# Half of a triangular inverse moved from GpSimd to VectorE, its stores and loads re-ordered, and one wait of the final loads changed

## The reference

```python
m = jnp.where(strict, jnp.einsum('nbhik,nbhjk->nbhij', kb, kc) * decay, 0.0)
rhs = jnp.concatenate([vc * bc[..., None], kb * jnp.exp(G)[..., None]], axis=-1)
sol = lax.linalg.triangular_solve(m + jnp.eye(C, dtype=m.dtype), rhs,
                                  left_side=True, lower=True, unit_diagonal=True)
...
y = y + jnp.einsum('tef,efd->td', act, p['w_exp_down'][gi])
...
x = x + hier_moe(rmsnorm(x, p['norm_ffn']), p)
return (rmsnorm(y_p, norm_final), ...)
```

## Time and profile before

| | us |
|---|---|
| runs: median (lowest to highest) | 1358.15 (1356.75 to 1359.48) |
| profiled execution: its time | 1358.79 |
| its span, first to last instruction | 1357.0 |
| busy: PE, PEld, DVE, ACT, POOL | 1266.0, 986.7, 480.5, 424.2, 217.6 |
| mean granted TensorE clock | 0.978 |

### The profile page before, as it was taken

How to read it: one execution, slowest core, us unless ns; L and a number is a source line. 1 busy time by engine, 2 the same in 40 slices (tenths; PEclk the granted TensorE clock), 3 DMA queues, 4 the chain that set the end, 5 groups by cost and what they waited for, 6 DMA issues and landing times.

```text
span 1357.0 us, 23622 instructions
## 1 busy us (share of the span) xinstructions
PE 1266.0 (93%) x10186; PEld 986.7 (73%) x10186; DVE 480.5 (35%) x798; ACT 424.2 (31%) x730; POOL 217.6 (16%) x295
## 2 busy tenths in 40 slices
PE   5999999999999999959999897999999999999996
PEld 4999997888999998859999796544445444444543
DVE  5441353433346656423344776211111111111113
ACT  5532225433243567513456552001001010110004
POOL 0450000000122212830111054010000001000003
PEclk9999999999999999979999997999999999999997
DMA  5234339441262134332113249799999999999987
GB/s 225 94 109 151 117 130 367 157 181 68 89 220 74 63 102 123 114 101 86 55 40 111 105 165 376 315 398 424 430 430 432 431 431 430 430 430 430 431 333 173
DMA packets 68521, 317.91 MB, mean 234 GB/s; under 512 B 30143, under 2 KB 38719, under 8 KB 45521
## 3 DMA queue, kind: packets, MB, share of 16 engines
q1 hardware_dynamic: 66137, 312.80, 59.1%
q0 software_dynamic: 2304, 3.94, 0.8%
HBM read 296.07 MB, written 25.10 MB: 237 GB/s over the span
## 4 chain that ended last, share of the span: by engine, by line
PE 64%; DMA 20%; DVE 5%; ACT 5%; POOL 2%; issue 2%; SPq 1%; POOLq 0%; ACTq 0%; DVEq 0%
PE pp L957 31%; DMA e_up<-in_w_up 17%; PE pp L1134 14%; PE pp L1123 3%; PE pp L1007 2%; DMA yt<-y_rows 1%; PE pp L1333 1%; DVE w_l L2108 1%; PE pp L1353 1%; PE pp L927 1%; POOL inv_s L1968 1%; POOL inv L1973 1%; PE pp L1361 1%; ACT w_h L1537 1%; DMA raw<-in_w_blk 1%
## 5 line engine op out<-in xcount | busy, mean ns | idle before, releaser
L957 PE MATMUL pp<-ht_h,w_h 128*128 128x260 f32 x1248 | 262.1, 291 | 0.6 <-DVE w_l L2108 0.6
L957 PE MATMUL pp<-ht_h,w_l 128*128 128x260 f32 x1248 | 252.3, 284 | 0.0
L957 PE MATMUL pp<-ht_l,w_h 128*128 128x260 f32 x1248 | 252.1, 284 | 0.0
L957 PEld LDWEIGHTS pp<-ht_h,w_h 128*128 128x128 f32 x1248 | 193.4, 190 | 5.0 <-issue 3.6
L957 PEld LDWEIGHTS pp<-ht_l,w_h 128*128 128x128 f32 x1248 | 193.4, 190 | 0.0
L957 PEld LDWEIGHTS pp<-ht_h,w_l 128*128 128x128 f32 x1248 | 193.4, 190 | 0.0
L2108 DVE TENSOR_TENSOR w_l<-raw,w_h 128x2048 fp32r<-128x2048 f32 x52 | 122.3, 2351 | 100.9 <-ACT w_h L1537 100.9
L1134 PE MATMUL pp<-e_up,xt 128*64 128x512 f32 x512 | 114.9, 602 | 16.7 <-DMA e_up<-in_w_up 16.7
L1123 PE MATMUL pp<-sel,h2p 104*128 104x128 bf16 x1920 | 114.7, 222 | 2.6 <-DVE sel L2560 2.6
L1537 ACT ACTIVATE w_h<-raw 128x2048 fp32r<-128x2048 f32 x52 | 99.6, 1916 | 47.4 <-PE pp L957 43.4
L1134 PE MATMUL pp<-e_gate,xt 128*64 128x512 f32 x512 | 112.6, 592 | 1.4 <-DVE xt L2607 1.4
(11 more groups left out here) (443 smaller groups left out, 1699.3 us busy)
## 6 DMA issues: line engine op xcount, KB each, us to landing
e_gate<-in_w_gate SPq DMA_DIRECT2D x15, 4096.0 KB, 20.8
e_down<-in_w_down SPq DMA_DIRECT2D x28, 2048.0 KB, 14.3
e_up<-in_w_up SPq DMA_DIRECT2D x14, 4096.0 KB, 22.6
raw<-in_w_blk SPq DMA_DIRECT2D x52, 1024.0 KB, 5.2
kv_ring<-in_cache_k SPq DMA_DIRECT2D x8, 1024.0 KB, 6.6
kv_ring<-in_cache_v SPq DMA_DIRECT2D x8, 1024.0 KB, 4.8
s_ring<-in_state_gdn SPq DMA_DIRECT2D x16, 512.0 KB, 5.0
e_up<-in_w_up SPq DMA_DIRECT2D x3, 2048.0 KB, 17.8
```

Source lines behind the costliest of these rows:

```text
L957: last = mm(dst, w_[:, k, cs], x_[:, k, ts], start=(k == 0 and q == 0), stop=(k == KD - 1 and q == 2))
```

## The change

- The column steps become two helpers, `column_product` and `column_out`, that either engine can issue. GpSimd keeps steps 0 to 14 (`SOLVE_SPLIT` is 15), VectorE does 15 to 30, three to five steps a gap, and turns the inverse right after the last one; `inv_turn` is no event any more.
- In `gap(0)` and `gap(1)` the solve now stands ahead of `conv_s` and `sd_u`; `zero` moves from `gap(2)` to `gap(1)`.
- SyncE asks for the first chunk's `m_t` rows between the two stores, waits for the first store alone before it loads blocks, loads the four of `t_lo` first, and those of `t_up` after the second store. `mt4` waits for `t_lo` alone, `tx4` for `t_up`, each by a count of its own (two old semaphores are used again, from 16 and from 32 on).
- The final row loads wait for `oh_mm` in place of `quarter_mm`.

```diff
-    gap(0, ("conv_s", 1), ("solve", 15, 18))
-    gap(1, ("sd_u",), ("solve", 18, 22))
-    gap(2, ("zero",), ("solve", 22, 26), ("turn_v", 0))
-    gap(3, ("solve", 26, 31), ("inv_turn",))
+    gap(0, ("solve", 15, 18), ("conv_s", 1))
+    gap(1, ("zero",), ("solve", 18, 22), ("sd_u",))
+    gap(2, ("solve", 22, 26), ("turn_v", 0))
+    gap(3, ("solve", 26, 31))
...
+        def column_product(tt, j):
+            n, m = 31 - j, j + 1
+            return tt(inv_s[:, 0:n * m].rearrange("p (n m) -> p n m", n=n),
+                      a32[:, j, j + 1:32].rearrange("p (n o) -> p n o", o=1).to_broadcast([128, n, m]),
+                      inv[:, j, 0:m].rearrange("p (o m) -> p o m", o=1).to_broadcast([128, n, m]), ALU.mult)
+
+        def column_out(tt, j):
+            n, m = 31 - j, j + 1
+            below = inv[:, j + 1:32, 0:m]
+            return tt(below, below, inv_s[:, 0:n * m].rearrange("p (n m) -> p n m", n=n), ALU.subtract)
...
-                sp.wait_ge(t_zero, 2 * c + 1)
-                for i, dst in ((1, t_up[c % 2]), (0, t_lo)):
-                    if i == 0:
+                sp.wait_ge(t_zero, 2 * c + (1 if c else 2))
+                for i, dst in ((1, t_up[c % 2]), (0, t_lo)) if c else ((0, t_lo), (1, t_up[0])):
+                    if c and i == 0:
                         sp.wait_ge(t_zero, 2 * c + 2)
+                    if not c and i == 1:
+                        sp.wait_ge(turn_stored, turn_from + 16)
...
                     sp.dma_start(inv_rows[0], inv[:]).then_inc(inv_stored, 16)
+                    load_chunk_rows(0)
                     sp.wait_ge(inv_done, SOLVED + 1)
-                    sp.dma_start(inv_rows[1], inv_t[:]).then_inc(inv_stored, 16)
+                    sp.dma_start(inv_rows[1], inv_t[:]).then_inc(turn_stored, 16)
...
-                        sp.wait_ge(inv_stored, 32)
+                        sp.wait_ge(inv_stored, 16)
...
             sp.wait_ge(y_free, rounds * NPAIR + 1)
-            sp.wait_ge(quarter_mm, rounds)
+            sp.wait_ge(oh_mm, rounds)
...
-                pe.wait_ge(t_loaded, 128 * (n + 1))
+                pe.wait_ge(t_loaded, 64 * (n + 1))
...
+                pe.wait_ge(up_loaded, up_from + 64 * (n + 1))
                 each(("tx4", n), fn)
...
-                elif e == "inv_turn":
-                    dve.wait_ge(inv_done, SOLVED)
-                    copy(inv_t[:], inv[:].rearrange("p i k -> p k i")).then_inc(inv_done, 1)
+                elif e == "solve" and ev[1] >= SOLVE_SPLIT:
+                    for j in range(ev[1], ev[2]):
+                        dve.wait_ge(inv_done, 2 * j)
+                        column_product(tt, j).then_inc(inv_done, 1)
+                        dve.wait_ge(inv_done, 2 * j + 1)
+                        column_out(tt, j).then_inc(inv_done, 1)
+                    if ev[2] == 31:
+                        dve.wait_ge(inv_done, SOLVED)
+                        copy(inv_t[:], inv[:].rearrange("p i k -> p k i")).then_inc(inv_done, 1)
```

More of the change, by code:

```diff
@@ L281 @@
 EU_EXTRA = 32
-SOLVED = 62
+SOLVED, SOLVE_SPLIT = 62, 15
 TOK_UNIT = (0, 1, 3, 0, 1)
@@ L545, in build_step @@
         t_zero, t_loaded = sem("t_zero"), sem("t_loaded")
+        up_loaded, up_from = mem_loaded, 16
+        turn_stored, turn_from = ws_loaded, 32
         m_loaded = [sem(f"m_loaded{i}") for i in range(2)]
@@ L711, in load_inverse, with load_chunk_rows @@
                         own = slice(32 * b + NH * c, 32 * b + NH * c + NH)
-                        sp.dma_start(dst[blk, :, blk], inv_rows[i, own].rearrange("h i k -> i h k")).then_inc(t_loaded, 16)
+                        sp.dma_start(dst[blk, :, blk], inv_rows[i, own].rearrange("h i k -> i h k"))\
+                            .then_inc(up_loaded if i else t_loaded, 16)
+            def load_chunk_rows(c):
+                sp.dma_start(m_t[c % 2][:], m_rows[NH * c:NH * c + NH].rearrange("h j i -> j h i"))\
+                    .then_inc(m_loaded[c % 2], 16)
             xk = a["x_t"].rearrange("p (k n) -> p k n", k=KD)
@@ L794, in _ @@
                     sp.dma_start(inv_rows[0], inv[:]).then_inc(inv_stored, 16)
+                    load_chunk_rows(0)
                     sp.wait_ge(inv_done, SOLVED + 1)
-                    sp.dma_start(inv_rows[1], inv_t[:]).then_inc(inv_stored, 16)
+                    sp.dma_start(inv_rows[1], inv_t[:]).then_inc(turn_stored, 16)
                 elif e == "t_load":
                     if ev[1] == 0:
-                        sp.wait_ge(inv_stored, 32)
+                        sp.wait_ge(inv_stored, 16)
                     load_inverse(ev[1])
-                elif e == "m_load":
+                elif e == "m_load" and ev[1]:
                     c = ev[1]
@@ L804, in _ @@
                         mmed(sp, ("ss", c - 2))
[L805 to L808, removed]
+                    load_chunk_rows(c)
                 elif e == "late_loads":
@@ L1202, in experts @@
                                 last.then_inc(y_mm, 1)
-                        if f == 0:
-                            last.then_inc(quarter_mm, 1)
                         if f == nf - 1:
@@ L1576, in tile @@
                     if t >= 5:
-                        act.wait_ge(inv_stored, 32)
+                        act.wait_ge(inv_stored, 16)
+                        act.wait_ge(turn_stored, turn_from + 16)
                     fn(whole(zg[:, t, :]), ps, ACT.Sigmoid, bias=param("b_gate", t + 8)).then_inc(free, 1)
@@ L1958, in _ @@
                     nc.gpsimd.memset(inv[:].rearrange("p i k -> p (i k)")[:, 0:1024:33], 1.0).then_inc(zeroed, 1)
-                elif e == "solve":
+                elif e == "solve" and ev[1] < SOLVE_SPLIT:
                     if ev[1] == 0:
```

10 lines of the change are left out of this document (2 added, 8 removed).

## The result

| | before | after |
|---|---|---|
| median of 4 runs beside each other, us | 1358.49 | 1342.26 (1340.09 to 1344.16) |
| ratio, 95% interval | | 0.9881 (0.986 to 0.9903) |
| profiled execution: time, span, us | 1358.79, 1357.0 | 1343.78, 1341.5 |
| mean granted TensorE clock | 0.978 | 0.987 |

The changed kernel is 16.2 us faster; 19.7 was forecast.

What follows compares the result with a forecast made beforehand. The chain was taken as 64% TensorE and 20% DMA, with re-ordering winning only at the wait for the inverse and the tail. Middle 14.4 plus tail 5.3 made 19.7 us: 1358.15 to 1338.5, range 1333 to 1347.

Steps and rivals of the forecast that it cites:

- The solve: Columns 15 to 30 on VectorE take 12.3 us; the inverse is finished at 581.3, 6.05 us before 587.35.
- the memsets wouldn't block the columns: GpSimd's three memsets beside VectorE's columns were taken at nothing; if they held VectorE up, 2.88 us.
- ScalarE's cover: ScalarE's exponentials, delayed 5.3 us, end at 584.95, just ahead of VectorE's a_t product at 585.05: covered by 0.1 us.
- The store and t_lo: Inverse's store lands 2.56 us after 581.3; the last lower block load, issued at 585.25, lands at 587.0, perhaps 588.
- The merge: First merge product on TensorE starts at 588.0 instead of 599.44, 11.4 us sooner.
- The clock: From the merge's start to 605.4 TensorE ran 6 us at half clock; 3.0 us more gained if the clock holds.
- The prediction's worry: TensorE's two new waits for ScalarE, 3 to 3.5 us each, may lower the clock; the second could cost about 2 us.
- Middle: From the solve through the merge, sooner merge start and held clock together give 14.4 us.
- The tail: Stored rows asked for sooner at the end move as a block from about 1315: 5.3 us, between 1.2 and 9.4.
- The named sign: If the last down product stretches beyond 7.1 us, stored rows and expert weights take turns on the queue.
- The slower rival: VectorE's column steps cost 2.4 times, as beside a GpSimd column; merge 8.4 us late, 1361.3 us; chance 0.04.

Runs made afterwards that it cites:

- e1: Changed kernel with the final row loads again waiting for the first quarter of the last down product (quarter_mm); 1346.03 us, 0.9894 of the kernel before.
- e6: Changed kernel with the store of the turned inverse moved behind the four t_lo loads; 1340.93 us, 0.9847 of the kernel before.
- e7: Changed kernel with each share of the stored rows loaded as 96 and 8 partitions instead of one load of 104; 1340.51 us, 0.9847 of the kernel before.
- e10: Changed kernel timed again, unchanged, in a later group of runs; 1340.86 us, 0.9862 of the kernel before.
- e2: Kernel before with the division of the columns alone, stores, loads and row request in the old order; 1350.0 us, 0.9931 of the kernel before.
- e9: Kernel before with unused products in TensorE's two waits, 90 before the sample norm's matmul and 28 before the merge; 1361.46 us, 1.0007 of the kernel before.
- e4: Changed kernel with the sample convolution ahead of columns 15 to 17 in VectorE's order; 1343.59 us, 0.9877 of the kernel before.
- e5: Changed kernel with the sample convolution ahead of the columns and 24 unused products in TensorE's wait before the sample norm; 1337.67 us, 0.9833 of the kernel before.
- e11: Changed kernel with convolution first, 24 unused products before the sample norm, and the turned inverse stored behind the t_lo loads; 1339.52 us, 0.9845 of the kernel before.
- e12: Kernel before with unused products in TensorE's two waits, 90 before the sample norm's matmul and 52 before the merge; 1357.04 us, 0.9973 of the kernel before.
- e8: Changed kernel with four 128x1024 products of x_mid by itself on GpSimd behind the three memsets; 1345.0 us, 0.99 of the kernel before.

## Why the prediction was right, point by point

- **The solve**: 15.6 us from column 14 to the finished inverse were forecast; it took 14.6. The seven small steps of the sample state took 1.7 us instead of 2.2, the columns and the convolution the rest less. (Rows 11 give 1.02 ns an element, not the 1.03 that I used; that is 0.1 us of it.) That the memsets wouldn't block the columns was right; that the turning's 1.63 held the price of a memset beside it I did not see.
- **ScalarE's cover** failed. It was to hold by 0.1 us; `a_t` waited 1.28, and 1.24 to 1.28 in e1, e6, e7 and e10. ScalarE was as late as forecast; VectorE, 1 us sooner with the inverse and 0.6 with the turning, came to it earlier. So this ate what VectorE won beyond the forecast: `a_t` is 6.4 us sooner relative to column 14, 6.1 were forecast.
- **The store and t_lo** were mis-sized: 3.21 and 3.47 us in the first trace instead of 2.56 and 1.75, the second with perhaps 1 us more for `inv_t`'s store. The store takes 3.1 to 3.2 in every trace in which the `m_t` rows are asked for 0.4 us behind it, and 2.6 where they are not (before, e2, e9): I took away the wait at one end of the queue and did not charge the transfer that I put in its place. The load takes 2.59 to 2.70 in e1, e4 and e5, so the 1 us for `inv_t`'s store was about right and the first trace's 3.47 is a long one; e11 gets the 1.75 back by moving that store.
- **The merge** then starts 10.9 us sooner after column 14 (11.4 forecast; 11.1 to 11.8 in e1, e7 and e10). That this came out is in part luck: the inverse, 1.1 us sooner than forecast, pays in the first trace for a store and a load that were each 0.6 to 0.7 longer.
- **The clock**: 3.0 forecast, 2.8 by e12 and by the merge's own rows. The prediction's worry, that TensorE's new waits for ScalarE might take the clock down and the second alone cost up to 2 us, came true in part. The first is 3.3 us long, the second 0.2 to 2.5, where 3 to 3.5 were estimated. In after, e1 and e6 the clock falls behind the first (0.70 at 576 to 580 in after), where TensorE only comes later to the next wait for ScalarE. In e7 and e10 it falls behind the second, and there the slow products do lead up to the merge: it starts 22.7 to 22.8 us after column 14, in e1 22.0. So that fall costs some 0.7 us. In none of these traces does it reach the merge itself. e4 shows what happens when the first wait is taken away.
- **Middle**: 13.7 in the profile, 13.7 to 14.6 over four traces, for 14.4.
- **The tail**: 5.3 forecast; 2.2 in the first trace, 5.1 over seven against six. The rows do start as a block when the weights are through (share 0.93 at 1300 to 1304), and come at 212 to 233 GB/s. Unseen was what is late next: when the rows come sooner, the adds and ScalarE's norms, 2.8 us a share, queue behind each other and become the end. The named sign, a last down product stretched beyond 7.1 us, came and went (a wait for the last quarter of the weights of 0.22 in after, 0.99 in e7 and 1.29 in e11, none in e4, e5, e6, e8 and e10, and none in the six traces with the old request), so rows and weights do seem to collide at times, but by little.
- **The slower rival** rested on a wrong price. It would have been decided not by a mean of 0.76 a step but by how many GpSimd instructions that read stand beside the columns, and how long each is (e8).

The gain was 16.2 and 19.2 in the two timings where 19.7 was forecast. Middle and tail by their means over the traces make 14 + 5 = 19; the first timing's lower figure fits a tail at its poor end, but no profile of its other runs shows that.

## What to carry to other kernels

When a step moves between engines that share a port, price it by what the other engine reads meanwhile, instruction by instruction. Removing a wait of the matrix engine can move its idle time to where the clock counts (e4): look where the idle time goes, and if it lands before work on the path, fill it. When a load is moved in a queue, charge its transfer to what now stands ahead of it and behind it.

## What the runs showed of the hardware that I had not expected

- Where the idle time stands can count for more than how much there is: with the same 16 products 1.8 us sooner but right behind idle time, the merge took 3.68 us instead of 2.00 and M grew by 2 (e4); products that nobody reads gave 3.7 us back (e5).
- The clock does not fall after every such wait: behind 3.30 us in after it did, behind 3.29 in e10 it did not; behind 2.52 in e10 it did, behind 2.50 in e2 it did not.
- The same load of stored rows runs at 190 to 207 GB/s before, 212 to 233 in the first trace of after and 250 to 283 in the second (stretches of 4 us), at a DMA share of about 0.8 most of the time; putting 16 engines on it instead of 13 changes the share and brings no rate outside this scatter (205 to 245 in e7). What sets it is open; I tried nothing that tells the places of memory apart.
- One two-input VectorE instruction of 0.23 us took 1.88 beside a GpSimd product of 1.98; memsets of 0.95 cost such steps nothing. The copy that turns the inverse took 1.63 to 1.70 where a memset ran beside it and 1.03 to 1.13 where none did.
